# Value pages loaded early and on two queues, two page pairs a head in the gated linear attention's output loop, and the first softmax inside that loop

## What is computed

```python
def page_step(carry, xs):                      # one of 8 pages of each sample
    k, v = mla_keys_values(cache_ckv_l[phys], cache_kpe_l[phys], kpos, w_ukv, g_kh)
    sc = jnp.einsum('bthd,bkhd->bhtk', q, k).astype(jnp.float32) * scale
    m_new = jnp.maximum(m, sc.max(axis=-1))
    p = jnp.exp(sc - m_new[..., None])
    ...
def step(s, inp):                              # GLA, one chunk of 64 tokens
    inter = jnp.einsum('bthk,bhkv->bthv', qc * jnp.exp(b), s)
    o = inter + jnp.einsum('bhts,bshv->bthv', att, vc)
    s = jnp.exp(bl)[..., None] * s + jnp.einsum('bshk,bshv->bhkv', kc * jnp.exp(bl[:, None] - b), vc)
```

## Time and profile before

| | us |
|---|---|
| median of 3 runs | 1036.35 |
| lowest, highest | 1035.65, 1038.83 |
| profiled execution, its own time | 1037.44 |
| its span, first to last instruction | 1035.5 |
| PE busy of it | 977.0 (94%) |
| PE's mean granted clock | 0.965 |

### The profile page before, as it was taken

How to read it: one execution, slowest core, us unless ns; L and a number is a source line. 1 busy time by engine, 2 the same in 40 slices (tenths; PEclk the granted TensorE clock), 3 DMA queues, 4 the chain that set the end, 5 groups by cost and what they waited for, 6 DMA issues and landing times.

```text
span 1035.5 us, 17055 instructions
## 1 busy us (share of the span) xinstructions
PE 977.0 (94%) x6576; PEld 872.2 (84%) x6576; DVE 573.5 (55%) x1042; ACT 435.0 (42%) x792; POOL 141.0 (14%) x238
## 2 busy tenths in 40 slices
PE   6999989979985889999999999999999999999997
PEld 5998468769875658999977777778899999999997
DVE  6443787777574436884430003359965866444454
ACT  6424456642244224674140004434765655333343
POOL 3442000000124340000310005920000000000000
PEclk9999989988688889999999999999999999999999
DMA  8447001211245443544342432050153544344441
GB/s 325 155 175 285 16 7 50 88 37 57 90 130 168 146 156 122 202 165 163 122 155 90 163 156 89 1 213 2 42 185 123 204 163 163 123 163 163 163 163 47
DMA packets 33762, 135.37 MB, mean 131 GB/s; under 512 B 5257, under 2 KB 16777, under 8 KB 21010
## 3 DMA queue, kind: packets, MB, share of 16 engines
q1 hardware_dynamic: 26786, 116.71, 30.7%
q0 software_dynamic: 6896, 17.58, 5.1%
HBM read 130.11 MB, written 4.17 MB: 130 GB/s over the span
## 4 chain that ended last, share of the span: by engine, by line
PE 80%; DVE 9%; issue 4%; ACT 2%; POOLq 1%; DMA 1%; POOL 1%; SPq 0%; DVEq 0%; ACTq 0%
PE ps L833 18%; PE ps L801 15%; PE ps L803 14%; PE ps L802 14%; PE ps L1007 2%; PE ps L1008 2%; PE ps L1009 2%; POOLq L635 1%; PE ps L1161 1%; PE ps L1117 1%; PE ps L930 1%; DVE const L2435 1%; POOL arena L566 1%; DMA ring<-in_stream 1%; DMA arena<-in_ckv 1%
## 5 line engine op out<-in xcount | busy, mean ns | idle before, releaser
L833 PE MATMUL ps<-arena,ring 128*128 128x288 f32 x512 | 124.3, 406 | 0.0
L833 PEld LDWEIGHTS ps<-arena,ring 128*128 128x128 f32 x512 | 97.2, 190 | 26.8
L801 PE MATMUL ps<-nhi_split,hi_split 128*128 128x288 f32 x320 | 95.1, 297 | 0.1
L1007 PE MATMUL ps<-sq_split,hT_split 128*128 128x256 f32 (+1 forms) x256 | 82.8, 324 | 12.1 <-DVE pages_lo_split L2022 7.0
L803 PE MATMUL ps<-nhi_split,ring_split 128*128 128x288 f32 x320 | 94.1, 294 | 0.0
L1872 DVE TENSOR_TENSOR ring_split<-ring,hi_split 128x2048 fp32r<-128x2048 f32 x36 | 82.2, 2285 | 17.4 <-ACT hi_split L1453 17.4
L1453 ACT ACTIVATE hi_split<-ring 128x2048 fp32r<-128x2048 f32 x36 | 68.7, 1910 | 31.2 <-PE ps L803 22.7
L2229 DVE TENSOR_TENSOR hT<-hT,ps 128x288 f32<-128x288 f32 x24 | 10.8, 452 | 126.7 <-PE ps L833 94.5
L1008 PE MATMUL ps<-wuk_lo_split,hT_split 128*128 128x256 f32 (+1 forms) x256 | 79.0, 308 | 0.0
L1009 PE MATMUL ps<-sq_split,pages_lo_split 128*128 128x256 f32 (+1 forms) x256 | 78.9, 308 | 0.0
L801 PE MATMUL ps<-up_nhi_split,up_hi_split 128*128 128x288 f32 x256 | 76.2, 298 | 0.1
(11 more groups left out here) (394 smaller groups left out, 2461.9 us busy)
## 6 DMA issues: line engine op xcount, KB each, us to landing
ring<-in_stream SPq DMA_DIRECT2D x97, 1024.0 KB, 4.9
arena<-in_ckvT SPq DMA_DIRECT2D x64, 128.0 KB, 2.1
arena<-in_ckv POOLq DMA_DIRECT2D x49, 128.0 KB, 2.6
arena<-in_wu POOLq DMA_DIRECT2D x1, 2240.0 KB, 9.0
arena<-in_s POOLq DMA_DIRECT2D x4, 512.0 KB, 3.5
out_gla_s<-arena POOLq DMA_DIRECT2D x4, 512.0 KB, 2.9
arena<-in_ckv SPq DMA_DIRECT2D x15, 128.0 KB, 2.9
hT<-in_x SPq DMA_DIRECT2D x2, 576.0 KB, 4.3
```

Of the source, the lines that this page charges most:

```text
L801: pe.matmul(ps[:, 0:T], wh[:, k, col:col + P], xh, start=first and k == which[0], stop=False)
L833: mm = pe.matmul(ps[base:base + m, 0:T], wv[:, k, col:col + m], rhs(k), start=first and k == which[0], stop=last and k == which[-1])
L1007: pe.matmul(out, hi, wuk_hi[:, k, cols], start=start, stop=False, skip_group_check=True)
```

## The change

- **Early pages.** The first 21 value pages go to 3 x 7 slots in ring slots 3, 4 and 0, which lie idle after the input projection. POOL loads them right after its `wuk_lo`. In return the units `out2`, `out3` and `up0_0` are now loaded by SP after `ol0`.
- **Groups on two queues.** Of the other 43 pages, 11 (`first`, needed by c = 0) and 23 (`second`) start after `gmix_ready` and the last state update, and 9 (`last`) after `ol0`; POOL takes the even and SP the odd places of each group.
- **Pair 0.** POOL instead of DVE makes the low parts of pairs 0 and 1; ACT rounds these two pages ahead of the keys' squares; on DVE the query columns come ahead of the `kh` products. Pair 1 moves ahead of the new tokens' scores.
- **More pairs early.** One more pair before `b`, and pairs 13 to 17 after it; on ACT and DVE pair 13 stands between the exponentials and products of the decays, and PE asks for `qb` (`gla_ready` 4) only at the samples' states.
- **Output loop.** Two pairs a head, 20 to 27; the halves of the second stand between `oss` and the two `su`, and its last heads behind them. DVE sums the second pair's squares ahead of its additions of `su`. `key_squares(0)` follows head 0, `key_factors(0)` head 1, `scaled_scores(0)` head 2.
- **After the loop.** Pairs 28 to 31 all stand before `weighted_values(0)`; after it come `out_linear(0)`, the maxima of c = 1, `latents_up(0)`, and so on.

```diff
@@ plan, and alike in the engines' blocks
     for h in range(GH):
-        main(("ka", 16 + h, 0), 2)
+        p = 20 + 2 * h
+        main(("ka", p, 0), 2)
         main(("go", h), 2)
-        main(("ka", 16 + h, 1), 2)
-        side(("kb", 16 + h))
+        main(("ka", p, 1), 2)
+        side(("kb", p))
         side(("oss", h))
+        main(("ka", p + 1, 0), 2)
         side(("su", h, 0))
+        main(("ka", p + 1, 1), 2)
         side(("su", h, 1))
+        side(("kb", p + 1))
@@ program
+        early_slots = [view(ring[U[n] % RING], 0, 7 * 257, s=7, n=257) for n in ("out2", "out3", "up0_0")]
+        def value_page(n):
+            return early_slots[n // 7][:, n % 7] if n < EARLY else cpages[:, (n - EARLY) % SLOTS]
+        first_pages = range(EARLY, half_pages)
+        second_pages = range(half_pages, EARLY + SLOTS)
+        last_pages = range(EARLY + SLOTS, NS * NPG)
@@ SP
             page_pairs(0, NP)
-            value_pages(sp, page, odd_pages, lambda n: values_in_odd)
+            sp.wait_ge(gmix_ready, GH)
+            copied(sp, ("su", GH - 1, 0))
+            copied(sp, ("su", GH - 1, 1))
+            value_pages(sp, page, first_pages[1::2], values_first[1])
+            value_pages(sp, page, second_pages[1::2], values_second[1])
             sp.wait_ge(side_ready, g.of[("kb", NP - 1)][2])
             sp.dma_start(hT[:, :], ins["x_by_step"]).then_inc(x_again, 16)
+            sp.wait_ge(main_ready, g.of["ol0"][2])
+            value_pages(sp, page, last_pages[1::2], values_last[1])
             weights(first, len(UNITS))
@@ POOL
+            for p in range(AHEAD):
+                pool.wait_ge(page_hi, p + 1)
+                pool.tensor_tensor(pages_lo[:, p % 4].rearrange("p j k n -> p (j k n)"), pages[:, p % 4].rearrange("p j k n -> p (j k n)"),
+                                   as_whole(pages_hi[:, p % 4].rearrange("p j k n -> p (j k n)")), ALU.subtract).then_inc(first_split, 1)
             pool.wait_ge(main_ready, g.of[("k", H - 1)][2])
...
+            for v in early_slots:
+                pool.memset(v[:, :, 256:257], 1.0).then_inc(value_ones, 1)
+            value_pages(pool, page, range(EARLY), values_early)
...
-            value_pages(pool, page, [n for n in range(NS * NPG) if n not in odd_pages], lambda n: values_in[n // 32])
+            value_pages(pool, page, first_pages[0::2], values_first[0])
+            value_pages(pool, page, second_pages[0::2], values_second[0])
+            pool.wait_ge(main_ready, g.of["ol0"][2])
+            value_pages(pool, page, last_pages[0::2], values_last[0])
@@ PE, the output loop
                 pe.wait_ge(vmask_ready, h + 1)
                 for c in range(2):
+                    first_heads(p + 1, c)
                     ps = bank(("su", h, c))
                     ready(pe.matmul(ps[:, :], ktok[0:TN, h, TP:TP + P], vmask[0:TN, 4 * c:4 * c + 4].rearrange("p b v -> p (b v)"),
                                     start=True, stop=True), ("su", h, c))
+                last_heads(p + 1, 0)
+                last_heads(p + 1, 1)
@@ ACT, the decays
-            act.activation(ebl, bT, ACT.Exp, scale=1 / 16).then_inc(decay_ready, 1)
             act.activation(kt, dT, ACT.Exp, scale=-1 / 16).then_inc(decay_ready, 1)
             act.activation(kd, kd, ACT.Exp, scale=1 / 16).then_inc(decay_ready, 1)
-            act.wait_ge(decay_ready, 1)
+            squared_keys(13, 14)
+            act.activation(ebl, bT, ACT.Exp, scale=1 / 16).then_inc(decay_ready, 1)
+            act.wait_ge(decay_ready, 3)
             act.activation(qt, dT, ACT.Exp, scale=1 / 16).then_inc(decay_ready, 1)
```

## The result

The changed kernel takes 1004.69 us (median of 4 executions, 1004.14 to 1007.03), the kernel before 1037.47 us in the same comparison: a ratio of 0.9689, with a 95% interval of 0.9665 to 0.9714. I had forecast 999.6 us, with a range of 993.0 to 1016.0; the gain was 32.8 us where I had summed up 36.7. The profiled execution has its own time 1004.14 us and a span of 1002.5 us.

What follows compares the result with a forecast made beforehand. The prediction took PE, busy for 94% of the span, as the bound, so only its waits and clock could give time. Gains of 6.5 + 3.2 + 13.0 + 14.0 = 36.7 us from 1037.44 gave 1000.7, median 999.6 us; range 993 to 1016.

Steps and rivals of the forecast that it cites:

- Part A: Ahead of pair 0: the 5.1 us wait for query columns and 2.0 us of half clock go; gain 6.5 us.
- Part B: At the decays after the gates: 6.1 us lost in place of 9.3; gain 3.2 us.
- the two branches: After the gates: a 3.4 us wait, then a second of 1.7 us, or none if pair 15 runs at half clock.
- Part C: Output loop: four heads with two pairs each at full clock, loop 49.7 us; gain 13.0 us.
- The order of the rivals: Output loop: full clock taken as forecast; clock falling all the same, 1019.5 us at full price, chance 0.15.
- Part D: After the loop: second sum of values 35.3 us after the loop's end in place of 50.0; gain 14.0 us.
- L: The end of the output loop, from which times behind it are counted; 293.60 us before the change.
- rival 2: After the loop: last pages land late, the three units served first, 6.7 us more, 1006 us; chance 0.10.
- rival 4: After the loop: DVE holds up POOL's issue of 23 late pages, 15.6 us, 1015 us; chance 0.02.

Runs made afterwards that it cites:

- `a_kh_first`: Changed kernel with the two `kh` products ahead of the query columns on DVE again, low parts of pairs 0 and 1 still on POOL: 1009.64 us.
- `b_sums_first`: Changed kernel with the squares and sums of pair 13 behind the first product of the decays in place of the second, on ACT and DVE: 1004.82 us.
- `c_one_pair`: Changed kernel with one page pair a head in the output loop, the other four after the loop ahead of the first sum of values: 1003.31 us.
- `c_pair_before_su`: Changed kernel with each head's second pair in one piece ahead of the two state updates, which stand side by side again: 1007.63 us.
- `d_units_wait`: Changed kernel with SP holding the three 1 MB weight units back until the last value pages have landed: 1004.13 us.
- `m_all2`: Changed kernel with two pairs moved behind the loop, 7 late pages on ACT, units held back, pair 13's sums earlier and scores split: 995.41 us.
- `d_both`: Changed kernel with ACT issuing 7 of the second pages and SP holding the weight units back until all pages have landed: 1001.18 us.
- `c_scores_split`: Changed kernel with the scores' eight products at the second head's end and only their maximum at the third's: 1004.01 us.

## Why the prediction was right, and where it was not

**Part A** was right: pair 0 starts at 141.76 us where I had PE ready at 141.67, without a wait and at full clock. `a_kh_first` shows its terms, 3.8 us for the order and 1.3 for the low parts, and the half clock behind them (1.3 us there, where I had taken 2.0).

**Part B** was right in size (5.8 us lost in place of 9.3: a wait of 3.30 us and 2.5 us of half clock; forecast 6.1), and the wait was worked out rightly as 3.4 us. But the 6.1 is not the middle of the two branches as I had them: they are 3.4 + 1.7 = 5.1 us at full clock and 3.4 + 2.3 = 5.7 at half, and the run took the second. That 6.1 came so close is partly luck. What I did not see is that the stretch is bound by DVE. That is why the clock there is worth 0.7 us and why an earlier low part is worth 0.9.

**Part C**: the clock held, as forecast, in every profile with the pair between the state updates but one (`b_sums_first`, where it was down for some 3.4 us at the third head's end). The step that was mis-sized is "a head at full clock with a second pair takes 8.93 + 3.1": it takes 12.44 us, since a pair in three pieces costs 3.5 us, and with the wait of 1.75 us (forecast 1.6) and a fourth head that is otherwise 0.25 us longer the loop is 51.75 and not 49.7 us. The order of the rivals was sound too: at the old place the clock does fall, in three heads before, in two in `c_one_pair` and in one in `c_pair_before_su`. Why it falls in one head and not in the next, no run shows, so the reason that I gave, products between the short ones, is borne out in tendency only.

**Part D**: the times up to the last issue were right. PE was ready for the second sum at L + 25.4 (26), the first sum ended at L + 18.8 (18.8), POOL's last page left at L + 30.6 (30.5). One step failed on the way, "so it does not wait": PE waited 1.98 us for the first pages, whose last one POOL issued at L + 11.3, later than I had it, and the shorter sum (4.2 us in place of the 5.8 I took) made it good, which was luck. The term that was mis-sized is the landing of the last page: 4.8 us by the earlier trace rows, measured 6.89. With it the end adds up: L + 30.63 + 6.89 + 0.46 to PE's start = L + 37.98, where I had L + 35.3; my outer bound of L + 38.5, for which I had given no row, just held. Here the timeline of SP behind the pages, and the landing times from 316 to 345 us:

```profile
319.36 0.43 SPq L632 DMA_DIRECT2D hT<-in_x_by_step  x1
320.55 3.81 SPq L579 DMA_DIRECT2D arena<-in_ckv  x4
```

```profile
ring<-in_stream SPq DMA_DIRECT2D x3, 1024.0 KB, 11.5
arena<-in_ckv POOLq DMA_DIRECT2D x12, 128.0 KB, 5.8
```

The units enter from 324.4 us on, the first of them ahead of POOL's last four pages, and `d_units_wait` shows that they are the difference: 3.10 us without them. So rival 2 was the right mechanism with too high a price. It had the pages served behind all three units, 6.7 us more; they shared the engines and lost 3.8. This is nearer to the rule of the Trainium skill, page "DMA: Bandwidth & Descriptors" (Queues, rings and completion order), by which each DMA engine takes turns between queues; the case agrees in that the page issued after 3 MB were queued landed in 6.89 us, while the units took 11.5.

**POOL's issue beside DVE** (rival 4) did not show: from the third on POOL's pages left every 1.14 us, with DVE busy for 18.3 of 38.0 us. The rule of the Trainium skill, page "SBUF — State Buffer" (SBUF: two separate sides), speaks of VectorE in a two-port mode; no run here shows whether any instruction in this stretch ran in one, so the rule is neither confirmed nor refuted.

**What the sum itself hid.** I added C and D as if they were apart. They are not: the second sum is tied to the loop's end by the pages, and PE waits 12.6 us ahead of it. Work in front of the loop's end costs its full length, and work behind it nothing, up to those 12.6 us. `c_one_pair` shows it from one side (a loop with the clock down in two heads, and the same time), `m_all2` from the other (two pairs moved behind the loop, together with earlier pages and scores, 11.5 us, where `d_both` with its edits of the pages gave 5.7). The forecast came within 5 us because the terms were taken in the order of the program, each against the stretch as it then stood, and not because each part is worth what its row says.

## What to carry to other kernels

When a wait ends with a transfer, find the event that lets the transfer start, and move work from in front of that event to behind it before making either faster; fill the wait first, then shorten it. A part that restores the clock is worth nothing while the time it saves ends in such a wait, so undo each part alone before crediting it. And among late transfers, hold back the large ones that nobody waits for yet until the small ones have landed, but see what their later use then waits for.

## What the runs showed of the hardware that I had not expected

- The same wait of 3.30 us at the same place was followed by half clock in the changed kernel and by full clock in `c_scores_split`. In `b_sums_first` the clock was down behind a wait of 2.03 us. The length of a pause does not settle what the clock does behind it.
- After the long wait for pages the clock came back at about 339.2 us in the changed kernel and in `d_units_wait`, though PE had resumed 3.0 us earlier in the second (335.54 against 332.58).
- Executions of one kernel differ by what the clock does: `c_pair_before_su` took 1002.45 us at a mean clock of 0.987 and 1014.66 us at 0.972. An edit worth 1 or 2 us is read from the profile's stretches, not from such medians.
- A 128 KB page landed in 3.10 us with two queues of pages and nothing else at the end, in 6.89 us with 3 MB of units on SP's queue beside it, and in 9.11 us with three queues of pages and the layer's input among them. A third queue bought 4.4 us alone, and 4.8 us together with the units held back, which alone bought 3.8.
